# A hybrid decoder step on one core: expert results of the prompt added straight into the output, decode rows by a scatter of their own

## What is computed

```python
x = x + MoE(RMSNorm(x))        # shared SwiGLU expert + top 8 of 64 routed SwiGLU experts

def routed_experts(h, eidx, gate_w, ...):
    # tokens are listed by expert, in blocks; for each block of tokens tok of expert e
    ys = swiglu(h_pad[tok], w_e_gate[e], w_e_up[e], w_e_down[e])
    out = zeros.at[row_tok].add(ys * row_w[:, None])
```

## Time and profile before

| | us |
|---|---|
| median of 3 runs | 2069.21 (2067.4 to 2072.2) |
| the profiled execution | 2082.22 |
| its span, first to last instruction | 2080.4 |
| PE busy | 1913.9 |
| DVE busy | 1317.7 |
| ACT busy | 997.0 |
| POOL busy | 784.6 |

### The profile page before, as it was taken

One profiled execution on the slowest core, in us unless ns is written; L12 is line 12 of the kernel. 1 busy time (PEld: TensorE's weight loads), 2 busy tenths in 40 slices (PEclk: granted clock), 3 DMA queues, 4 the chain that ended last, 5 costly groups with the idle time before them and its releaser, 6 DMA issues. The chain is left out here.

```text
span 2080.4 us, 38308 instructions
## 1 busy us (share of the span) xinstructions
PE 1913.9 (92%) x13128; PEld 1493.0 (72%) x13128; DVE 1317.7 (63%) x2150; ACT 997.0 (48%) x1537; POOL 784.6 (38%) x672
## 2 busy tenths in 40 slices
PE   7999799968799999999898978999999999999994
PEld 5788778856456588888687536777777777777773
DVE  4389767776689731111567527777777777777772
ACT  6322123366576621111343106776766676676672
POOL 2111033353445210111026513446644565565452
PEclk9999899989899999999999999999999999999997
DMA  7488831065577859870623147999999999999995
GB/s 238 138 294 266 267 119 42 19 199 181 187 225 229 273 192 302 259 227 21 240 93 121 53 188 281 354 342 353 351 342 355 349 335 344 348 343 355 338 342 142
DMA packets 170944, 501.88 MB, mean 241 GB/s; under 512 B 26326, under 2 KB 71956, under 8 KB 144396
## 3 DMA queue, kind: packets, MB, share of 16 engines
q1 hardware_dynamic: 128164, 353.65, 46.7%
q0 software_dynamic: 31680, 80.82, 15.4%
q10 hardware_dynamic: 10992, 66.02, 9.5%
HBM read 437.87 MB, written 120.75 MB: 269 GB/s over the span
## 5 line engine op out<-in xcount | busy, mean ns | idle before, releaser
L2770 DVE TENSOR_TENSOR w_gu_lo<-turned,w_gu_hi 128x2048 fp32r<-128x2048 f32 x132 | 302.6, 2293 | 102.1 <-ACT w_gu_hi L2684 100.4
L2684 ACT ACTIVATE w_gu_hi<-turned 128x2048 fp32r<-128x2048 f32 x132 | 252.5, 1914 | 43.2 <-PEq L1932 43.2
L2532 POOL DMA_INDIRECT x_scratch<-turned,target x66 | 144.7, 2192 | 289.3 <-DMA x_scratch<-turned,target 248.3
L668 PE MATMUL pP<-wring,hT_hi 128*128 128x512 f32 (+2 forms) x520 | 205.8, 396 | 17.8 <-DVE wring L594 6.4
L2607 PE MATMUL pG_e<-w_gu_hi,xT_hi 128*128 128x512 f32 x528 | 216.7, 410 | 0.0
L2607 PE MATMUL pG_e<-w_gu_lo,xT_hi 128*128 128x512 f32 x528 | 210.1, 398 | 0.0
L2607 PE MATMUL pG_e<-w_gu_hi,xT_lo 128*128 128x512 f32 x528 | 209.7, 397 | 0.0
L670 PE MATMUL pP<-wring,hT_lo 128*128 128x512 f32 (+2 forms) x520 | 200.9, 386 | 0.0
L669 PE MATMUL pP<-wring,hT_hi 128*128 128x512 f32 (+2 forms) x520 | 200.8, 386 | 0.0
L2793 DVE TENSOR_TENSOR w_e_lo<-turned,w_e_hi 128x2048 fp32r<-128x2048 f32 x66 | 151.1, 2289 | 20.8 <-ACT w_e_hi L2698 20.8
L412 POOL TENSOR_TENSOR wring<-turned,wring 128x512 fp32r<-128x512 f32 (+1 forms) x43 | 69.7, 1647 | 224.0 <-ACT wring L448 223.8
(11 more groups left out here) (354 smaller groups left out, 4623.8 us busy)
## 6 DMA issues: line engine op xcount, KB each, us to landing
turned<-in_w_e_up SPq DMA_DIRECT2D x65, 1024.0 KB
turned<-in_w_e_down SPq DMA_DIRECT2D x65, 1024.0 KB
turned<-in_cache_sb_kv SPq DMA_DIRECT2D x256, 256.0 KB, 3.3
turned<-in_w_e_gate SPq DMA_DIRECT2D x64, 1024.0 KB
out<-in_cache_win_kv ACTq DMA_DIRECT2D x8, 4094.0 KB
turned<-in_w_in ACTq DMA_DIRECT2D x56, 256.0 KB, 6.4
turned<-in_w_in SPq DMA_DIRECT2D x16, 512.0 KB, 7.7
out<-in_cache_win_kv ACTq DMA_DIRECT2D x8, 1022.0 KB
```

Source lines behind the costliest of these rows:

```text
L668: pe.matmul(pP[:m, b, :w], hi, w_hi(u), start=(c == 0), stop=False)
L2532: pool.indirect_dma_start(sc["x2"], bass.IndirectOffsetOnAxis(ap=target[:, j, 0:1], axis=0), y[j], None, bounds_check=T - 1, oob_is_err=Fa ...
L2684: act.activation(ghi[:, r, k, :, :].rearrange("p c f -> p (c f)"), w[:, r, k, :], ACT.Copy).then_inc(ghi_ready, 1)
L2770: dve.tensor_tensor(glo[:, r, k, :, :].rearrange("p c f -> p (c f)"), w[:, r, k, :], ghi[:, r, k, :, :].rearrange("p c f -> p (c f)").bitc ...
```

## The change

The prompt rows are no longer gathered in `sc["x2"]`. SP stores residual plus shared expert of the eight prompt tiles directly into the first output, and only the decode rows into the scratch. Each main scatter and each tail scatter adds into the first output, with the bound at the last prompt row, so that decode rows are skipped. Behind each main scatter stands a second one of the block's first 8 rows, which adds into `sc["x2"]` (prompt rows among the 8 are added there too, where nobody reads them). It has its own semaphore, `decode_out`, 16 for each; the small scatter waits for the one of the block before, and ACT's `put` waits for it before it overwrites `y[j]`. At the end only the 8 decode rows are copied.

```diff
@@ -1974,7 +1974,8 @@
                 for t in range(NT):
                     m = rows_of(t)
                     sp.wait_ge(x2_ready, t + 1)
-                    sp.dma_start(sc["x2"][t * P:t * P + m, :], x2[:m, t % 2, :]).then_inc(x2_out[t % 2], 16)
+                    dst = o[0][0, t * P:t * P + m, :] if t < NP else sc["x2"][S:T, :]
+                    sp.dma_start(dst, x2[:m, t % 2, :]).then_inc(x2_out[t % 2], 16)
@@ -2387,7 +2388,7 @@
-    x2_quarters = sc["x2"].rearrange("t (q n) -> (t q) n", q=QT)
+    out_quarters = o[0][0].rearrange("t (q n) -> (t q) n", q=QT)
@@ -2444,11 +2445,8 @@
         y_copied = sem("e_y_copied")
+        decode_out = sem("e_decode_out")
         copied = sem("c_copied")
-
-        def half_rows(ap, h):
-
-            return ap[h * (S // 2):(h + 1) * (S // 2), :].rearrange("(p n) d -> p (n d)", p=P)
@@ -2500,10 +2498,9 @@
                 load_down(last, SHORT)
-                sp.wait_ge(y_out, last * 48 + 48)
+                sp.wait_ge(decode_out, last * 32 + 32)
                 sp.dma_start(o[1][:, 0], sc["x2"][S:T, :]).then_inc(copied, 16)
-                sp.dma_start(half_rows(o[0][0], 0), half_rows(sc["x2"], 0)).then_inc(copied, 16)
-                sp.wait_ge(copied, 48)
+                sp.wait_ge(copied, 16)
@@ -2529,13 +2526,18 @@
                         pool.wait_ge(y_out, it * 48 + 32 * j)
                     pool.wait_ge(y_copied, it * 3 + 2 * (j == SHORT) + 1)
                     pool.nop(nofuse=True)
-                    pool.indirect_dma_start(sc["x2"], bass.IndirectOffsetOnAxis(ap=target[:, j, 0:1], axis=0), y[j], None,
-                                            bounds_check=T - 1, oob_is_err=False, compute_op=ALU.add).then_inc(y_out, 16)
+                    pool.indirect_dma_start(o[0][0], bass.IndirectOffsetOnAxis(ap=target[:, j, 0:1], axis=0), y[j], None,
+                                            bounds_check=S - 1, oob_is_err=False, compute_op=ALU.add).then_inc(y_out, 16)
+                    if seen(it, j, 1):
+                        pool.wait_ge(decode_out, it * 32 + 16 * j)
+                        pool.nop(nofuse=True)
+                    pool.indirect_dma_start(sc["x2"], bass.IndirectOffsetOnAxis(ap=target[:NS, j, 0:1], axis=0), y[j][:NS, :], None,
+                                            bounds_check=T - 1, oob_is_err=False, compute_op=ALU.add).then_inc(decode_out, 16)
                     if j == LONG:
                         pool.wait_ge(y_copied, it * 3 + 2)
                         pool.nop(nofuse=True)
-                        pool.indirect_dma_start(x2_quarters, bass.IndirectOffsetOnAxis(ap=target[:, j, 1:2], axis=0), y_tail, None,
-                                                bounds_check=QT * T - 1, oob_is_err=False, compute_op=ALU.add).then_inc(y_out, 16)
+                        pool.indirect_dma_start(out_quarters, bass.IndirectOffsetOnAxis(ap=target[:, j, 1:2], axis=0), y_tail, None,
+                                                bounds_check=QT * S - 1, oob_is_err=False, compute_op=ALU.add).then_inc(y_out, 16)
@@ -2721,6 +2723,7 @@
                     if seen(it, j, 2):
                         act.wait_ge(y_out, it * 48 if j == SHORT else it * 48 - 16)
+                        act.wait_ge(decode_out, it * 32 if j == SHORT else it * 32 - 16)
@@ -2756,9 +2759,6 @@
                 put(last, SHORT)
-                act.wait_ge(y_out, last * 48 + 48)
-                act.dma_start(half_rows(o[0][0], 1), half_rows(sc["x2"], 1)).then_inc(copied, 16)
-                act.wait_ge(copied, 48)
```

## The result

The changed kernel takes 2111.58 us (median of 4 runs, 2105.91 to 2118.82), the kernel before beside it 2070.7 (4 runs, 2067.4 to 2078.26): a ratio of **1.0187, 95% interval 1.0158 to 1.0215**. It is slower, as forecast, but by 41 us where 17.6 were forecast, and 2111.6 lies outside the range of 2060 to 2108.

The account below looks back on a forecast made before the run. Bound: PE, busy 92%, at balance with POOL, whose scatters wait for landings and make gathers late. Loop +28.6 us (13 stalls, 41 us, less 12.6), end -11: +17.6 on a 2069.2 median, 2087 us; range 2060 to 2108.

Parts of the forecast that it names:

- the new waits and the bytes: Expert loop: waits of POOL and ACT's copies on the small scatters' semaphore, and 2.1 MB added, each put at nothing.
- The end: After the last scatter: only the 32 KB decode copy is left on SP, 3.5 us; gain 11 us, bounds 9 and 13.
- The small scatter's price: POOL in the expert loop: each small scatter costs 0.85 + 0.30 = 1.15 us, two a round 2.3 us.
- The 1.9 for LONG's from above: Upper bound for LONG's small scatter ahead of the tail's: 1.15 us plus a mean wait for VectorE's subtraction, 1.9 us.
- The balance of stalls: Expert loop: PE's 23.63 + 3.15 f equals POOL's 24.4 + a - (2.6 - 1.2) f; f = 0.42, 13 stalls, +28.6 us.
- the earlier cliff: Gather behind SHORT's small scatter: turns late 1.15 us earlier in the round; a stall gives POOL 1.2 us less lead back.
- One that meets none takes 1.07: POOL's gathers: one starting inside VectorE's subtraction takes 2.96 us, one that meets no subtraction 1.07.
- Rival 1: Expert loop: small scatters hidden, four to six stalls, loop costs 0 to 6 us, end wins 11: 2058 to 2064; chance 0.22.
- Rival 3: Expert loop: every round stalls, 3.15 us each, +74, 2143 us; chance 0.08 for over two thirds of the rounds.
- the draw: Whole kernel: a near 0.3 with the earlier cliff costs +10 against the end's -11, 2065 to 2073; chance 0.12.
- No room on POOL: Kernel before is at a balance point: POOL's round about 24.4 us against PE's 23.6, four stalls in 31 rounds.
- C: Experiments' theory for the expert loop: POOL's time costs wherever it stands; relieving the changed kernel gives 2052 to 2070 us.

Follow-up runs that it names:

- e1_no_small: Changed kernel without the 66 small scatters and the waits on their semaphore: 0.9961 of the kernel before, 2061.3 us against 2069.2.
- e4_plain_small: Changed kernel with small scatters that write instead of adding, same rows, bytes and waits: 1.0098 of the kernel before, 2087.9 us.
- the multiplication: Changed kernel with a POOL multiplication, no transfer, in place of each small scatter: 344 columns (0.75 us added) 1.0068, 584 columns (1.14 us) 1.0108 of the kernel before.
- y2_zeros_rows_skipped: Changed kernel whose small scatters add zeros from their own tile, nearly all rows skipped, without ACT's wait for them: 1.0127 of the kernel before.
- e7_gap: Changed kernel with LONG's small scatter behind the tail's and SHORT's ahead of its main scatter: 1.0199 of the kernel before, 2110.9 us.
- x1_rows_skipped: Changed kernel with the small scatter's bound at 0, so nearly all its rows are skipped, waits kept: 1.0144 of the kernel before.

## Why the prediction was wrong

Its direction and its mechanism (a late gather behind POOL's work) held. One term of the sum was mis-sized, and two that it put at nothing, the new waits and the bytes, were something.

- **The end**: 11 us forecast, bounds 9 and 13; 11.1 measured in the profiled executions, some 8 (3 to 13 by the interval) by `e1_no_small`. SP's copy takes 2106.7 - 2102.78 = 3.9 us to the end, forecast 3.5. Right.
- **The small scatter's price, the step that failed.** "Eight rows are few, so I take 0.85 + 0.30 = 1.15 us": the row that I took it from is an 8-row scatter that writes, and this one adds. Adding costs 1.34 to 1.39 us, with the 0.30 before it 1.65, and 1.88 with the time for which VectorE holds it back (1.58 + 0.30). The bound from above, the adding scatter of 1.59, was the nearer relative. The 1.9 for LONG's from above was right in size, though its own working, 1.15 + 0.58 x 1.15, gives 1.82. `e4_plain_small` shows this: with the forecast's instruction the loop loses 27 us, the forecast's 28.6. That run also changes what the transfer does at its target, but the multiplication of nearly the same dose loses the same.
- **The balance of stalls** holds with the right price in it. With a = c = 1.65 for the added time and the earlier cliff, f = (0.77 + 1.65) / (3.15 + 2.6 - 1.65) = 0.59, 18 stalls, 57 us, less 12.6 = +45; the trace has 17 long rounds and +51.1. The rest is in the price of one: 63.7 / 17 = 3.75 us where 3.15 was taken. The plain wait is 48.6 / 17 = 2.9 us of it, against 10.4 / 4 = 2.6 before. Why a stall costs more isn't shown; in the round above the tail's scatter and the copies are held by two subtractions one after the other (1509.20 to 1513.8), but I didn't count how often.
- **Both small scatters count**, as forecast: LONG's by 1.17% and SHORT's by 1.07%.
- **"The new waits ... nothing"** was wrong: ACT's `put` waited 8 times for a small scatter (16.7 us). Without that wait and without the bytes the ratio falls by 0.60% (half-width 0.51), some 12 us, and I had named just such a wait as what would refute me. It is a smaller part, not the cause. The 15 waits of `put` for a main scatter are not of this kind: they are still 15 in `y2_zeros_rows_skipped`.
- **"One that meets none takes 1.07"**: the gather of 2.96 us is right, but it is so long because it starts within the subtraction (1492.57, the subtraction from 1492.30 on the earlier trace rows). In the kernel before, all 62 gathers that don't start within one take 1.01 to 1.08 us, whether or not one begins during them. So a transfer pays for VectorE only when it starts within a subtraction; the mean wait in the 1.9 is of that kind.
- **Rival 1** (hidden, and faster) had for it the 237.4 us in which POOL only waited for landings. That idle time was no cover: it stands ahead of the main scatter, while the small scatter and the gathers stand behind it, and `e7_gap`, which aimed a small scatter at it, only got it behind the landing. Rival 3's two thirds of long rounds were not reached (17 of 31), but it was nearer than the draw.
- **"No room on POOL"** was half right. More POOL time costs at once, 1.07% for the first 0.75 us a block; but less of it gives nothing in the kernel before (0.9999), where POOL's longest waits are for landings. The balance formula, with 0.8 us less on POOL, has no stall left and wins all of the 12.6 us (0.6%) that were there to win; the interval allows 0.3%. So the formula holds for added time only, and why isn't settled.
- **The range's** upper end rested on a = 1.9 for LONG's alone, with an earlier cliff of 1.2. Price and cliff are the same instruction and had to be moved together; with 1.9 in both the formula gives +55, and with the end's 11 us off 2113.

What stays open: how far landings and order set the pace, since the loop doesn't give back what C says when POOL is relieved; how the 0.6% of the bytes and of ACT's wait divide between the two, and whether POOL's time at the full dose costs just the 1.66% of the zeros with rows skipped, since the multiplication stopped at 1.14 us.

## What to carry to other kernels

Before you add a small instruction to an engine that looks idle, ask whether its idle time lies ahead of a wait for a transfer or behind it, and what stands in order behind the new one. Price an indirect transfer by its kind (adding or writing) as much as by its rows: here eight rows added cost POOL 1.36 us and a hundred and twenty-eight 1.58. And when an experiment replaces an instruction by a stand-in, measure the dose on the timeline, as the distance between its two neighbours, before reading the ratio: the mean duration put the multiplication above the small scatter (1.86 against 1.58 us), where its dose is less than half.

## What the runs showed of the hardware

- An indirect transfer's time on POOL, undisturbed: 0.92 us for 8 rows of 4 KB written (`e4_plain_small`), 1.34 to 1.39 us for 8 rows added, 1.58 us for up to 128 rows added. With nearly all rows past the bound it is still 1.34 us (`x1_rows_skipped`). About 0.30 us lie between two that follow each other.
- VectorE's subtraction of two tensors of 128x2048 (2.29 us) holds back an indirect transfer that starts within it: the 19 such small scatters of the changed kernel end 1.22 to 1.26 us behind the subtraction's end. One that starts earlier isn't slowed: the other 47 take 1.34 to 1.39 us, one of them 1.37 us with a start only 0.10 us ahead of the subtraction. The Trainium skill (SBUF — State Buffer, Who interferes with whom) says that a VectorE instruction with two SBUF inputs contends with a GpSimd instruction that reads SBUF, and infers that descriptor generation does not wait for such an operation. The trace agrees with the inference as far as a transfer under way goes (1.37 us). That what is held at the start is the reading of the row numbers from SBUF would follow from the page's rule; no run here shows it apart.
- A POOL operation on SBUF that follows an indirect transfer starts 0.5 us before the transfer's record ends (1543.80 against 1544.31), while a second indirect transfer starts 0.3 us after it. So the two kinds of instruction don't add up alike.
